# A transformer forward pass on one core: squares summed on VectorE, scores copied by bank, h seeded into the experts' sums

## What is computed

```python
for i in range(DEPTH):                       # 2
    f1 = swiglu(rmsnorm(h, g[0]), ...)       # feed-forward, width 2816
    h = h + FFN_RES * rmsnorm(f1, g[1])
    hn = rmsnorm(h, g[2])
    m = neighborhood_attention(hn, ...) if i % N_MIXERS == 0 else diff_attention(hn, ...)
    h = h + rmsnorm(m, g[3])
    f2 = swiglu(rmsnorm(h, g[4]), ...)
    h = h + FFN_RES * rmsnorm(f2, g[5])
return h[:, N_META:]
```

```python
s = jnp.einsum('nhpc,hpkc->nhpk', q, sub_keys)
s_top, i_top = lax.top_k(s, PEER_TOPK)
...
act = jax.nn.gelu(jnp.einsum('tkd,td->tk', u_emb[eb], tb), approximate=False) * gb
return jnp.einsum('tk,tkd->td', act, v_emb[eb])
...
x = x + _peer(_rmsnorm(x, norm2_g), ...)
return _rmsnorm(x, final_g)
```

## Time and profile before

| | |
|---|---|
| median of 3 runs | 2329.22 us (2326.59 to 2330.06) |
| profiled execution | 2329.45 us |
| its span, first to last instruction | 2327.7 us |
| TensorE busy, weight loads | 2237.0 us (96%), 2103.1 us (90%) |
| VectorE, ScalarE, GpSimd busy | 1641.1, 1040.9, 110.3 us |
| mean granted TensorE clock | 0.984 |

### The profile page before, as it was taken

The page is one execution under the profiler, slowest core; times in us unless marked ns, Lnnn a source line. Parts: engine busy times, 40 slices in busy tenths (PEclk is TensorE's granted clock), DMA queues, the critical chain, the costliest instruction groups (busy, mean ns, idle before and its releaser), DMA issues. The chain is left out here.

```text
span 2327.7 us, 45798 instructions
## 1 busy us (share of the span) xinstructions
PE 2237.0 (96%) x18076; PEld 2103.1 (90%) x18076; DVE 1641.1 (71%) x3090; ACT 1040.9 (45%) x1693; POOL 110.3 (5%) x42
## 2 busy tenths in 40 slices
PE   7999999999999998999799998989999999999997
PEld 7999789999999787999789988989999998888886
DVE  5665768765765676875586577699889965777775
ACT  5444455444444355544353344344444444333333
POOL 0000000000000000000000000089000000000000
PEclk9999999999999999999899999999999999999999
DMA  5553535553555442556231225445444454555553
GB/s 189 176 195 133 172 110 163 175 198 126 181 180 185 139 146 100 163 183 208 92 126 66 99 80 178 137 145 172 145 140 142 138 169 165 191 192 193 189 191 134
DMA packets 99244, 361.09 MB, mean 155 GB/s; under 512 B 11496, under 2 KB 15224, under 8 KB 98944
## 3 DMA queue, kind: packets, MB, share of 16 engines
q1 hardware_dynamic: 99072, 358.64, 45.9%
HBM read 357.55 MB, written 1.05 MB: 154 GB/s over the span
## 5 line engine op out<-in xcount | busy, mean ns | idle before, releaser
L949 DVE TENSOR_TENSOR w_lo<-ring,w_hi 128x1024 fp32r<-128x1024 f32 (+1 forms) x304 | 396.7, 1307 | 225.6 <-ACT w_hi L750 224.9
L750 ACT ACTIVATE w_hi<-ring 128x1024 fp32r<-128x1024 f32 (+1 forms) x304 | 340.7, 1125 | 373.1 <-PE ps L448 342.7
L448 PE MATMUL ps<-x_hi,w_hi 128*128 128x272 f32 (+1 forms) x1568 | 454.3, 290 | 2.1 <-issue 1.0
L448 PE MATMUL ps<-x_hi,w_lo 128*128 128x272 f32 (+1 forms) x1568 | 451.1, 288 | 0.0
L448 PE MATMUL ps<-x_lo,w_hi 128*128 128x272 f32 (+1 forms) x1568 | 449.5, 287 | 0.0
L448 PEld LDWEIGHTS ps<-x_hi,w_hi 128*128 128x128 f32 x1568 | 295.3, 188 | 4.0 <-issue 1.9
L448 PEld LDWEIGHTS ps<-x_lo,w_hi 128*128 128x128 f32 x1568 | 295.4, 188 | 0.1
L448 PEld LDWEIGHTS ps<-x_hi,w_lo 128*128 128x128 f32 x1568 | 295.4, 188 | 0.0
L234 ACT ACTIVATE v_gated_hi<-ring 128x1024 fp32r<-128x1024 f32 x128 | 135.8, 1061 | 216.0 <-PE ps L2992 215.2
L2779 PE MATMUL ps<-tok_hi,u_mid_hi 128*128 128x256 f32 x736 | 213.6, 290 | 1.3 <-POOL u_mid_lo L240 1.3
L2779 PE MATMUL ps<-tok_hi,u_mid_lo 128*128 128x256 f32 x736 | 208.1, 283 | 0.0
(11 more groups left out here) (497 smaller groups left out, 5129.8 us busy)
## 6 DMA issues: line engine op xcount, KB each, us to landing
ring<-in_gate_up SPq DMA_DIRECT2D x176, 512.0 KB, 3.3
ring<-in_peer_v SPq DMA_DIRECT2D x128, 512.0 KB, 3.2
ring<-in_peer_u_mid SPq DMA_DIRECT2D x92, 512.0 KB, 3.3
ring<-in_down SPq DMA_DIRECT2D x64, 704.0 KB, 4.0
ring<-in_w_in SPq DMA_DIRECT2D x46, 512.0 KB, 3.3
ring<-in_peer_u_early SPq DMA_DIRECT2D x36, 512.0 KB, 3.3
ring<-in_project SPq DMA_DIRECT2D x32, 512.0 KB, 4.2
ring<-in_na_qk SPq DMA_DIRECT2D x16, 512.0 KB, 4.0
```

The lines of the kernel that those rows point to most:

```text
L448: mm = nc.tensor.matmul(ps[:, bank, 0:ntok], parts[left][:, slot, t * P:(t + 1) * P], rhs[right][:, k, 0:ntok], start=start and n == 0, st ...
L750: A.activation(parts[0][:, n % SLOTS, 0:width[n]], ring[:, n % SLOTS, 0:width[n]], ACT.Copy).then_inc(hi_done.sem, 1)
L949: V.tensor_tensor(parts[1][:, n % SLOTS, 0:width[n]], ring[:, n % SLOTS, 0:width[n]], parts[0][:, n % SLOTS, 0:width[n]].bitcast(F32), ALU ...
```

## The change

1. Boundaries 2, 3 and 5: no sums between the k steps. DVE adds the eight squares in two wide adds behind its last rest (`gather_h_at_once`), and TensorE makes the eps sum and two sums behind item 3. ACT makes the high parts of the next items ahead of the Sqrt instead of behind it.
2. Boundaries 1 and 4: `inverse` goes to q/k slot 1, the eight `lower` to slots 2 to 9. Since `std` is now read later, `warm` (an activation that only loads a table) writes to another column.
3. Scores: ACT first makes the high parts of expert items 0 and 1, then copies the second scores bank by bank, each as it is complete.
4. `peer_v`: TensorE first multiplies h by the identity into banks 0 to 3, and the experts' sums go on top. `final_g` is loaded at the Block's start into free columns of `ring`. ACT takes a root of one column there. The last item signals after each token half, and the norm reads PSUM: square with sum, root, reciprocal, product. The two Blocks behind `peer_v` go.

```diff
+
+        def gathered_by(b):
+
+            return sum(KD - 1 if n in (1, 4) else 2 for n in range(1, b + 1))
...
-            def h_sum_gathered(b, nth):
-                pe.wait_ge(h_gathered, (KD - 1) * (nth + 1))
-                sum_of(7, sq[:, 0, 0:stream(b)[1]], False, True).then_inc(h_summed, 1)
+            def h_sum_gathered(b):
+                ntok = stream(b)[1]
+                eps_sum(b)
+                pe.wait_ge(h_gathered, gathered_by(b))
+                if b in (1, 4):
+                    sum_of(7, sq[:, 0, 0:ntok], False, True).then_inc(h_summed, 1)
+                else:
+                    sum_of(7, sq[:, 0, 0:ntok], False, False)
+                    sum_of(7, sq[:, 1, 0:ntok], False, True).then_inc(h_summed, 1)
...
-                    if k:
+                    if k and b == 0:
                         h_sum(b, k - 1)
-                    elif b:
-                        eps_sum(b)
...
-                h_sum(b, KD - 1)
+                if b == 0:
+                    h_sum(b, KD - 1)
...
                     whole_item(n0 + i, i % 6, ntok, x)
+                    if i == 3 and b:
+                        h_sum_gathered(b)
...
                     if item == 3:
-                        eps_sum(b)
-                        h_sum_gathered(b, i)
+                        h_sum_gathered(b)
...
             def warm(func):
-                A.activation(std[:, 0:1], eps, func)
+                A.activation(h[:, 0, T:T + 1], eps, func)
...
-                if b in (1, 4):
+                if b:
                     for n in range(n_next + 1, n_next + 1 + ahead_of(b)):
                         split_hi(n)
                 act.wait_ge(h_summed, b + 1)
@@ -794,7 +804,7 @@
                     A.activation(inv_h[:, 0:ntok], ps[:, 7, 0:ntok], ACT.Sqrt, scale=1.0 / D).then_inc(h_std, 1)
                 else:
                     A.activation(inv_h[:, 0:ntok], ps[:, 7, 0:ntok], ACT.Sqrt, scale=1.0 / D, bias=eps).then_inc(h_std, 1)
-                if b not in (1, 4):
+                if b == 0:
                     for n in range(n_next + 1, n_next + 1 + ahead_of(b)):
                         split_hi(n)
 
...
-                    done = (KD - 1) * (b // 4) + k - 1
+                    done = gathered_by(b - 1) + k - 1
...
+            def gather_h_at_once(b):
+
+                ntok = stream(b)[1]
+                dve.wait_ge(h_squared, KD * (b + 1))
+                V.tensor_tensor(sq[:, 0:4, 0:ntok], sq[:, 0:4, 0:ntok], sq[:, 4:8, 0:ntok], ALU.add).then_inc(h_gathered, 1)
+                dve.wait_ge(h_gathered, gathered_by(b) - 1)
+                V.tensor_tensor(sq[:, 0:2, 0:ntok], sq[:, 0:2, 0:ntok], sq[:, 2:4, 0:ntok], ALU.add).then_inc(h_gathered, 1)
...
                 if b in (1, 4):
                     gather_h(b, KD - 1)
-                    inverse(b)
+                elif b:
+                    gather_h_at_once(b)
                 for n in range(n_next + 1, n_next + 1 + ahead_of(b)):
                     split_lo(n)
...
                     split_lo(n0 + item + 4)
-                    if item < 7:
-                        for k in range(2 * item - 6, 2 * item - 4):
-                            lower(b, k)
...
                 for slot in range(21 if local else 20):
                     if slot < 16:
                         take_qk(slot)
+                    if slot == 1:
+                        inverse(b)
+                    if 2 <= slot < 2 + KD:
+                        lower(b, slot - 2)
                     if 0 <= slot - 2 < UNITS:
                         soften(slot - 2)
...
-
-                pe.wait_ge(score_kept.sem, 1)
+                        if tb == 1 and n % 4 == 3 or n == SETS - 1:
+                            mm.then_inc(scored.sem, 1)
+
+                pe.wait_ge(score_kept.sem, 4)
                 pe_linear(pe, w, u_parts, x_parts, KD, SEQ, 4, bank0=4)
 
                 for s in range(MID):
...
 
-                A.activation(second_score[:, :, :].rearrange("p (b s) k -> p b (s k)", b=4), ps[:, 4:8, :],
-                             ACT.Copy).then_inc(score_kept.sem, 1)
+                for i in range(2):
+                    take_hi(act, w, u_parts, i, i, 0)
+
+                for n in range(4):
+                    act.wait_ge(scored.sem, n + 2)
+                    A.activation(second_score[:, 4 * n:4 * n + 4, :].rearrange("p s k -> p (s k)"), ps[:, 4 + n, :], ACT.Copy).then_inc(score_kept.sem, 1)
                 for i, slot, turn in grouped(act, w.n, SLOTS):
-                    take_hi(act, w, u_parts, i, slot, turn)
+                    if not early(i, 2):
+                        take_hi(act, w, u_parts, i, slot, turn)
                     if not early(i, 2):
                         take_gelu(i - 2, (slot - 2) % SLOTS)
                 mid_hi(0)
```

In `peer_v`, with the two Blocks behind it removed:

```diff
+
+            room = gate_map[:, 0:20, :].rearrange("p j t -> p (j t)")
+            x_out, squares, small = room[:, 0:2 * D], room[:, 2 * D:4 * D], room[:, 4 * D:4 * D + 8]
+            final_g = ring[:, :, D:D + SEQ]
+            final_half, final_sq, final_std, final_inv, finished = flags("final_half", "final_sq", "final_std", "final_inv", "finished")
...
+                    sp.dma_start(final_g, a["final_g"].rearrange("p (s c) -> p s c", s=SLOTS)).then_inc(loaded.sem, 16)
                     load_stage(sp, "peer_v")
+                    for tb in range(2):
+                        sp.wait_ge(finished.sem, tb + 1)
+                        sp.dma_start(out[P * tb:P * tb + P, :], x_out[:, D * tb:D * tb + D]).then_inc(stored.sem, 16)
+                    sp.wait_ge(stored.sem, stored.at(32))
...
+                    A.activation(ring[:, 0, D + SEQ:D + SEQ + 1], col("eps", 0), ACT.Sqrt)
                     for i, slot, turn in grouped(act, w.n, SLOTS):
                         take_hi(act, w, parts, i, slot, turn)
+                    for tb in range(2):
+                        act.wait_ge(final_half.sem, tb + 1)
+                        A.activation(squares[:, D * tb:D * tb + D], ps[:, 2 * tb:2 * tb + 2, :].rearrange("p b n -> p (b n)"), ACT.Square,
+                                     accum_out=small[:, tb:tb + 1]).then_inc(final_sq.sem, 1)
+                        act.wait_ge(final_sq.sem, tb + 1)
+                        A.activation(small[:, 2 + tb:3 + tb], small[:, tb:tb + 1], ACT.Sqrt, scale=1.0 / D, bias=col("eps", 0)).then_inc(final_std.sem, 1)
 
...
+                    dve.wait_ge(loaded.sem, loaded.at(16))
+                    for tb in range(2):
+                        dve.wait_ge(final_std.sem, tb + 1)
+                        V.reciprocal(small[:, 4 + tb:5 + tb], small[:, 2 + tb:3 + tb]).then_inc(final_inv.sem, 1)
+                        dve.wait_ge(final_inv.sem, tb + 1)
+                        by_slot = lambda t: t.rearrange("p (s c) -> p s c", s=SLOTS)
+                        V.scalar_tensor_tensor(out=by_slot(x_out[:, D * tb:D * tb + D]), in0=by_slot(ps[:, 2 * tb:2 * tb + 2, :].rearrange("p b n -> p (b n)")),
+                                               scalar=small[:, 4 + tb:5 + tb], in1=final_g, op0=ALU.mult, op1=ALU.mult).then_inc(finished.sem, 1)
...
+
+                    for tb in range(2):
+                        for hf in range(2):
+                            for m in range(4):
+                                nc.tensor.matmul(ps[:, 2 * tb + hf, P * m:P * m + P], h[:, 4 * hf + m, P * tb:P * tb + P], ident[:, :], start=(m == 0), stop=False,
+                                                 skip_group_check=True)
+
+                    def expert_sum(j, b, final):
...
-                        mm.then_inc(mm_done.sem, 1)
+                            if final:
+                                mm.then_inc(final_half.sem, 1)
+                        if not final:
+                            mm.then_inc(mm_done.sem, 1)
```

64 lines of the change are left out of this document (6 added, 58 removed).

## The result

| | before | after |
|---|---|---|
| median | 2329.64 us (4 runs, 2326.59 to 2330.1) | 2311.17 us (4 runs, 2307.18 to 2314.32) |
| profiled execution | 2329.45 us | 2310.88 us |
| its span | 2327.7 us | 2309.1 us |

The ratio is 0.9921, 95% interval 0.9909 to 0.9933: the change takes 18.5 us off. The forecast was 2315.9 us with a range from 2311.8 to 2320.6. The side was right; the time came 4.7 us under the forecast and 0.6 us under the range.

A forecast was written before the change was run, and what follows sets the result against it. TensorE, busy 2237.0 of 2327.7 us, was taken as the bound, with its waits and what follows its last matmul. -4.4 - 1.2 + 1.4 - 0.2 - 9.2 = -13.6 from 2329.45 gave 2315.9 us, range 2311.8 to 2320.6.

The forecast's parts named there:

- A: Feed-forward norms at boundaries 2, 3 and 5: nine fp32 sums become three; -4.4 us, between 0 and -4.6.
- Rival 4: TensorE waits for x or `w_lo` at the feed-forward boundaries, so nothing is gained there; 2320.3 us, chance 0.10.
- B: Boundaries 1 and 4: reciprocal and eight `lower` moved into q/k slots, v ready sooner; -1.2 us, between +5 and -1.4.
- Rival 5: DVE becomes the bound of the q/k slots and scattered waits lower the clock; 2352 us, chance 0.02.
- C: Warm-up activation writes to another column: same instruction, zero.
- D: Scores copied bank by bank: TensorE's lead ends waiting for DVE's expert selection, then low clock; +1.4 us, between -1.2 and +1.7.
- Rival 1: The clock stays up at the transposes behind the selection, making the score step -1.2 us; 2313.3 us, chance 0.15.
- rival 2: TensorE's early start at the scores gets through to the end, -7.3 us, needing faster selection; 2307.2 us, chance 0.03.
- E1: Entry to the experts' sums: table load shifts the start, h's matmuls fill the idle; -0.2 us, between -0.4 and +1.5.
- Rival 3: Experts' entry dearer: clock low despite h's matmuls, 2317.6 us, chance 0.08; or a drain behind the table load, 2317.3, 0.04.
- E2: The end: final norm read from PSUM shortens the path behind the last expert matmul; -9.2 us, between -8.4 and -9.6.

The follow-up runs named there:

- x1: The kernel before with only the changed feed-forward norms of boundaries 2, 3 and 5; 2325.23 us, ratio to before 0.9981.
- x4: The changed kernel with one copy of all scores, as before, instead of bank by bank; 2313.2 us, ratio to before 0.9927.
- x3: The kernel before with only the new `peer_v` (h turned into the experts' sums, final norm out of PSUM); 2320.0 us, ratio to before 0.9956.
- x9: The changed kernel without the sixteen matmuls that turn h ahead of the experts' sums (output lacks h); 2316.21 us.
- x12: The changed kernel with `EARLY` = 44 instead of 36 and ACT's gelu one item later; 2298.62 us, ratio to before 0.9870.
- x6: The changed kernel with two more unused 128x1024 subtractions on GpSimd behind its last one; 2320.11 us.
- x2: The kernel before with only the moved `inverse` and `lower` and the warm-up's other column; 2329.0 us, ratio to before 0.9997.
- x11: The changed kernel with `EARLY` = 40 instead of 36 and ACT's gelu one item later; 2304.12 us, ratio to before 0.9888.
- x5: The changed kernel run again, unedited; 2312.07 us, ratio to before 0.9925.
- x7: The changed kernel with 36 unused fp32 matmuls of 128x128 on TensorE ahead of its wait for VectorE's selection; 2314.41 us.
- x10: The changed kernel without the one-column root at the entry to the experts' sums, so the root's table loads at the end; 2311.13 us.

## Why the prediction missed its range

**A, forecast -4.4, measured -4.8.** The mechanism is right, but the number came near because two errors offset each other. I took 0.26 us for a sum, from its start to the next group. But the matmul behind an fp32 sum takes longer as well. The k steps show the full price: in the kernel before seven of them lie between 574.36 and 585.48, 1.589 us each; without sums, timeline of the changed kernel, boundary 3,

```profile
569.71 0.53 PE L525 MATMUL ps<-x_lo,w_hi 128*128 128x272 f32 x3
...
574.72 0.54 PE L525 MATMUL ps<-x_lo,w_hi 128*128 128x272 f32 x3
...
575.84 0.55 PE L525 MATMUL ps<-x_lo,w_hi 128*128 128x272 f32 x3
...
578.22 0.53 PE L525 MATMUL ps<-x_lo,w_hi 128*128 128x272 f32 x3
...
581.93 0.62 PE L457 MATMUL ps<-inv_h,ones 128*128 128x272 f32 x2
582.39 1.08 PE L457 MATMUL ps<-sq,ones 128*128 128x272 f32 x4
583.10 0.49 PE L452 MATMUL ps<-x_hi,w_hi 128*128 128x272 f32 x1
583.43 0.29 PE L452 MATMUL ps<-x_lo,w_hi 128*128 128x272 f32 x1
```

seven take 8.51. A step in which nothing is held up takes 1.12 (574.72 to 575.84), so a lone sum costs 0.46 us: 0.26, and 0.2 at the matmul behind it (0.33 to the next one instead of 0.13). Nine are 4.1, and the three in a row cost 1.17 and 0.2: 2.8 less. But the loop without sums is held up for x in small pieces, some 0.65 us in these seven steps, and 0.32 for `w_lo` behind them, which the forecast had at nothing at this boundary: that leaves 1.8, where the landmarks have 1.85 and the forecast had 1.56. At boundary 5 the wait for `w_lo` stands as forecast:

```profile
938.60 0.39 PE L452 MATMUL ps<-x_hi,w_hi 128*128 128x256 f32 x1 [0.24 <-DVE w_lo L959]
```

Rival 4 (A is 0) is refuted by x1, though the waits that it asked for exist: they take back about a third.

**B, forecast -1.2, measured about -0.7.** At the first attention 0.7 was won. At the second the wait ahead of the q/k items fell from 0.97 to 0.27, so the same was won there, but it is not found again at boundary 5. The scatter covers it: the step takes 154.06, 154.24 and 155.68 us without B and 153.83 to 154.94 with it, and a new wait of 0.2 us for `probs` stands in the slots. Rival 5 (DVE the bound of the slots) is out: in 34 us of slots VectorE is busy for 27.85, and TensorE for 33.79.

```profile
818.00:852.00 34.00, 33.79 (x254) 29.66 (x253) 27.85 (x80) 19.93 (x58) 0.00 (x0) 1.00 0.41 147
```

**C, forecast 0.** Nothing in the traces speaks of a cost; it was only run together with B.

**D, forecast +1.4, measured -1.5: the step that failed.** The forecast said that TensorE's lead "doesn't reach the end", that the transposes need a chain "which no edit moves" and that VectorE's can shorten "only by its 0.94 us wait". TensorE did wait, for 9.6 us, and the clock was low behind it: that part held. But the chain has a partner. The edit moved POOL ahead by some 7 us, 11 by its last subtraction, and POOL's subtractions had been lengthening VectorE's compares and products. The trace of the kernel before had it to be read: two prices, 2.29 and 4.35, for one form. A mean over the form hides them. By the means of the nine profiles named under x4 the selection got 3.05 us shorter instead of 1.2, and the step behind it at low clock 1.55 us longer instead of 2.6. So of the 2.9 us between forecast and measurement 1.85 are the selection and 1.05 the clock, which came back after 3 to 5 us of work and not after 6. TensorE's own lead was underrated too, without an effect on D: it reached the transposes 13 us ahead and not 7.3, since most of its later waits for POOL went as well. Rival 1 (the clock stays up) and rival 2 (the early start gets through) did not come about, though rival 2 looked at the right quantity: it asked for a faster selection and was dismissed since "the change touches none of its instructions".

**E1, forecast -0.2, measured about -0.8** (-0.65 in x3, -0.95 in after). The forecast added the table load (1.5 us) to the entry; it came out at 1.0 to 1.4 us, since h's matmuls, ending at 1951.89, and `v_gated_lo` are through at the same time. The gain at full clock was 1.6 us over the first item and 1.6 to 2.1 over all items, instead of 1.7. x9 shows what it hangs on. Rival 3 is refuted in both halves.

**E2, forecast -9.2, measured -9.2.**

The landmarks thus give -4.8 - 0.7 - 1.5 - 0.8 - 9.2 = -17.0, so 2312.4 from the same starting point of 2329.45. The profiled execution of after is 1.6 us below that, having led by 1.9 at boundary 1 already. How much of the last 1 to 2 us of the median's difference is more than scatter stays open. The sum of the landmarks lies inside the range, so that the median fell outside owes as much to chance as to D; but D's own range (-1.2 to +1.7) was missed. It was too narrow for one reason: I let D go no lower than the -1.2 of rival 1, as if the sum of two waits were a bound on what a moved engine can do.

## What to carry to other kernels

Before calling a chain untouched, look at the engines that run beside it, not only at those that feed it: where one form of instruction has two durations in a timeline, look for an engine that works beside the longer one: here moving that partner moved the chain. Price a removed matmul by the period of the loop around it, not by its own record, and ask what it was hiding. And a new wait of a bottleneck engine is an offer: it showed where eight items of work could go, worth 12 us more in x12 by the medians.

## What the runs showed of the hardware

- A compare or product of VectorE with two SBUF inputs of 128x2048 takes 2.29 us alone, or where it starts 0.06 us ahead of a GpSimd subtraction with two SBUF inputs (kernel before, at 1612.59), and 4.31 to 4.54 where it starts while one runs (before, after, x6, x9). The subtraction goes from 2.39 to between 3.9 and 4.5 (8.39 for two). A reduction with one input takes 2.29 either way (x6), but a cast of 128x256 with one input takes 0.29 (x2) to 2.41 us (before).
- Behind waits of 5.0, 5.4, 5.8, 9.6 and 13.7 us (x9, before, x11, after, x6) TensorE's clock was at 0.50 (1.2 GHz). It came back 4.5, 5.9, 5.5, 3.1 and 5.7 us after work began; behind the same 9.6 us it took 2.7 in x9 and 5.0 in x5, and behind 5.4 us 3.1 in x4. Behind one of 1.5 us (x7) it was at 1.00 (2.4 GHz).
- An fp32 matmul of 128x272 between split products costs 0.46 us in the k loop (steps of 1.589 us with it and 1.12 without), where the trace has 0.26 from its start to the next one.
- A table load costs 1.28 us on ACT with 0.01 to 0.02 us to the activation behind it (x10).
